# Mixer stage: the square of the state-space output behind the next chunk's decays, and GpSimd's steps in another order

## Chip, cores and metric

The program runs on one core of one Trainium2 chip. The metric is the device time of one execution in microseconds (us), the median of several runs.

## What is computed

The reference is one layer of a hybrid network over 2048 tokens of width 1024. A projection gives q, k, v, z, xbc and dt. From these a dilated attention over three patterns and a state-space mixer are formed. Their outputs go through an output projection, a convolved gated feed-forward net and a gated embedding. The change lies in the state-space mixer, which works in 16 chunks of 128 tokens, with 16 heads of width 64 in 2 groups, and a state of 128:

```python
acum = jnp.cumsum(ac, axis=2)
decay = jnp.exp(jnp.where(causal, acum[:, :, :, None] - acum[:, :, None], -jnp.inf))
cb = jnp.einsum('bclgn,bcsgn->bclsg', cc, bc)
y_diag = jnp.einsum('bclsge,bcsgep->bclgep', cb[..., None] * decay, xc)
chunk_states = jnp.einsum('bclgn,bclgep->bcgepn', bc, xc * decay_to_end[..., None])
# over the chunks: h = h * chunk_decay + chunk_state
y_off = jnp.einsum('bclgn,bcgepn->bclgep', cc, h_in) * jnp.exp(acum)[..., None]
y = y_diag + y_off + d_skip[:, None] * xs
y = y * silu(z)
return rms_norm(y, norm_g)
```

The norm at the end needs the sum of y squared over the 1024 inner channels of each token.

## The kernel before, in words

The kernel has six stages: input projection, mixers, output projection, up projection, down projection and gated embedding. `mixers` (L1502) runs two programs side by side, `Attention` (L593) and `Ssd` (L1101). Each engine has a generator of each program. A generator yields a due time ahead of each group of instructions, and `weave` (L585) issues next whatever has the smallest due time. So the order in each engine's queue is fixed at build time by a plan. A group whose due time is smaller than one already issued from the same generator follows at once. An engine executes its queue in order; a semaphore wait holds all that is behind it.

**The plan.** In `Ssd`, `at(c, x)` (L1147) is 10 + 23.5 (c + x), in microseconds of the plan, so a chunk c has 23.5. In `Attention` there are four rounds r, with a first pass (maxima of the scores, 32 each) and a second pass (exponentials and value products, 75 each), in the order of L609: first passes 0 and 1, second 0, first 2, second 1, first 3, second 2 and 3. A second pass has 40 steps; step k is due at k/43 of its 75 on TensorE and at (k + 0.6)/43 on ScalarE (L842). Real time runs slower than the plan: the 16 chunks take about 35 us each.

**One chunk c of the mixer.**

- ScalarE: sixteen decays, one per head (L1288, Relu of the row of cumulative sums minus its own), after each eight of them an exponential of the group (L1293, made of 1024 columns), due from c - 0.5 on. The copy of B in token order (L1299) out of PSUM, which waits for TensorE's transposes (`turned_b`), is due at c - 0.28. The square of y (`square`, L1310, with L1314) waits for y_out and for GpSimd's additions of the chunk before, and is due at c + 0.64. In `scalar` the square of chunk c stands ahead of the decays of chunk c + 1 (due from c + 0.5).
- TensorE: `turn` (L1442) transposes x and B and forms the products of C and B (L1454, L1461, L1463), due at c - 0.32 and c - 0.2. `outputs` (L1466) forms the part from the state (L1476) and the part inside the chunk (L1485). `states` (L1488, product L1498) forms the chunk's state out of xde and the B copy, due at c + 0.9 and c + 0.98.
- VectorE: `front` (L1364) scales x by dt (L1373), masks the C-B product (L1380) and multiplies it into the decays (L1384). `outcome` (L1387) scales and adds the two parts (L1394, L1398; the second raises y_add). `carry` (L1400, L1407) adds the chunk's state to the decayed one; it is queued behind the next chunk's `front`.
- GpSimd (`gpsimd`, L1215): xde, which is x dt times the decay to the end (L1240); D times x into y (L1248), which waits for the store of the last y, for its square (sq_s) and for x; the decay of the state (L1254); y plus the sum of the two parts (L1259); y times z (L1262, raises y_out); and `add_up` (L1224), three halving additions of the squares (L1230), which waits for the square.
- SP's queue (`sync`, L1153): the load of x of chunk c + 2, which waits for D times x (dx_s, L1189) and for TensorE; the load of the cumulative rows of chunk c + 2; y's store (L1204, after y_out); z and e_cum of later chunks. The attention's loads stand in the same queue.

**Attention on the same engines.** In a second pass each step has two or more score products on TensorE (L1044 to L1046, L1049 to L1053) into one of two PSUM banks, an exponential on ScalarE (L849) and value products (L1077 to L1097). The score of step g waits for the exponential of step g - 2, the value products for the last exponential they read. The sums of a value step are added by VectorE (L928 to L936). In a first pass VectorE takes maxima (L886, L892) and ScalarE has nothing to do.

At the end TensorE sums the squares over the channels (L1438), which waits for all 16 `add_up`, and ScalarE takes the root (L1306).

Of the kernel before, what the change touches and what calls it, by code (L numbers as in the profile page):

```python
# [5 lines left out]
ALU = mybir.AluOpType  # L6
# [6 lines left out]
P = 128  # L13
SEQ, D = 2048, 1024
KD = D // P
TT = SEQ // P
# [3 lines left out]
SH, SP_, SN, SG = 16, 64, 128, 2  # L20
# [84 lines left out]
class Norm:  # L105
# [43 lines left out]
    def scalar(self, act, w_hi, w_in_s, whi_done):  # L149
        self.high_weights(act, 0, w_hi, w_in_s, whi_done)  # L150
        act.wait_ge(self.param, 16)
        for n in range(NB):
            if n == 0:
                act.wait_ge(self.first_in, 16)
            for k in range(KD):
                if k == (KD // 2 if n == 0 else 0):
                    act.wait_ge(self.loaded[n % 2], 16 * (n // 2 + 1))
                act.activation(self.hi[:, k, n * 512:(n + 1) * 512], self.x[n % 2][:, k], ACT.Copy,
                               scale=self.g[:, k:k + 1]).then_inc(self.hi_done, 1)
            if n == 0:  # L160
                self.high_weights(act, 1, w_hi, w_in_s, whi_done)
            else:
                self.take_root(act, n - 1)
            act.activation(self.sq[:, :, :], self.x[n % 2][:, :, :], ACT.Square).then_inc(self.squared, 1)
        self.take_root(act, NB - 1)
# [935 lines left out]
class Ssd:  # L1101
# [113 lines left out]
    def gpsimd(self, pool):  # L1215
        yield self.at(0, -1.6)
        pool.memset(self.one[:, :], 1.0).then_inc(self.consts, 1)
        pool.memset(self.state[0][:, :, :], 0.0).then_inc(self.consts, 1)
        pool.memset(self.eps[:, :], EPS).then_inc(self.consts, 1)
        pool.wait_ge(self.consts, 3)  # L1220
        pool.affine_select(out=self.upper[:, :], in_=self.one[:, :], compare_op=ALU.is_ge, fill=0.0, base=0,
                           pattern=[[1, P]], channel_multiplier=-1).then_inc(self.consts, 1)

        def add_up(c):  # L1224
            pool.wait_ge(self.sq_s, c + 1)
            for n, half in enumerate((4, 2, 1)):
                if c + n > 0:
                    pool.wait_ge(self.added, 3 * c + n)
                out = self.y_sq[:, 0:half] if half > 1 else self.y_sums[:, c * P:(c + 1) * P].unsqueeze(1)
                pool.tensor_tensor(out, self.y_sq[:, 0:half], self.y_sq[:, half:2 * half], ALU.add).then_inc(self.added, 1)  # L1230

        for c in range(TT):
            b = c % 2
            yield self.at(c, 0.04)
            pool.wait_ge(self.xdt_s, 2 * c + 2)
            if c > 0:
                pool.wait_ge(self.st_mm, 2 * c)
            else:
                pool.wait_ge(self.par_s, 1)
            pool.tensor_tensor(self.xde[:, :, :], self.xdt[b][:, :, :],  # L1240
                               self.to_end[:, c].unsqueeze(2).broadcast_to([P, SH, SP_]), ALU.mult).then_inc(self.xde_s, 1)
            yield self.at(c, 0.1)
            pool.wait_ge(self.xbc_in[b], 16 * (c // 2 + 1))
            pool.wait_ge(self.param, 64)
            if c > 0:
                pool.wait_ge(self.stored, 16 * c)
                pool.wait_ge(self.sq_s, c)
            pool.tensor_tensor(self.y[:, :, :], self.xbc[b][:, 0:INNER // P],  # L1248
                               self.d_col[:, :].unsqueeze(2).broadcast_to([P, INNER // P, P]), ALU.mult).then_inc(self.dx_s, 1)
            yield self.at(c, 0.2)  # L1250
            if c > 0:
                pool.wait_ge(self.state_s, 2 * c)
                pool.wait_ge(self.off_mm, 2 * c)
            pool.tensor_tensor(self.state[1 - b][:, :, :], self.state[b][:, :, :],  # L1254
                               self.chunk_decay[:, c].unsqueeze(2).broadcast_to([P, SH, SP_]), ALU.mult).then_inc(self.decayed_s, 1)
            yield self.at(c, 0.56)
            pool.wait_ge(self.y_add, 2 * c + 2)
            pool.wait_ge(self.dx_s, c + 1)
            pool.tensor_tensor(self.y[:, :, :], self.y[:, :, :], self.e_cum[b][:, :, :], ALU.add).then_inc(self.dy_s, 1)  # L1259
            pool.wait_ge(self.z_in, 16 * c + 16)  # L1260
            pool.wait_ge(self.dy_s, c + 1)
            pool.tensor_tensor(self.y[:, :, :], self.y[:, :, :], self.z[:, :, :], ALU.mult).then_inc(self.y_out, 1)  # L1262
            yield self.at(c, 0.7)
            add_up(c)

    def scalar(self, act):
        yield self.at(0, -1.4)
        act.wait_ge(self.vec, 2)
        act.activation(self.work[1], self.work[1], ACT.Exp, scale=-1.0).then_inc(self.act_s, 1)
        act.activation(self.row[:, 1], self.row[:, 1], ACT.Exp).then_inc(self.act_s, 1)  # L1270
        yield self.at(0, -1.0)
        act.wait_ge(self.cum_s, 3)
        act.activation(self.e_t, self.ps_y[:, 0:2], ACT.Exp).then_inc(self.rows_s, 1)
        act.activation(self.cum[:, :, :], self.ps_b[:, 0:2].rearrange("p a (c h) -> p (a c) h", h=SH), ACT.Copy
                       ).then_inc(self.act_s, 1)
        act.activation(self.chunk_decay[:, :, :], self.ps_o[:, 0:2].rearrange("p a (c h) -> p (a c) h", h=SH), ACT.Exp
                       ).then_inc(self.act_s, 1)
        yield self.at(0, -0.9)
        act.wait_ge(self.vec, 21)
        act.activation(self.to_end[:, :, :], self.work[2].rearrange("p (c h) -> p c h", h=SH), ACT.Exp).then_inc(self.par_s, 1)  # L1280
        for c in range(TT):
            b = c % 2
            for h in range(SH):
                if h % 2 == 0:
                    yield self.at(c, -0.5 + 0.02 * h)
                if h == 0:
                    act.wait_ge(self.cum_in[b], 16 * (c // 2 + 1))
                last = act.activation(self.m_t[b][:, h], self.m_t[b][:, h], ACT.Relu, scale=-1.0, bias=self.cum[:, c, h:h + 1])  # L1288
                if h % self.HG == self.HG - 1:
                    g, (heads, _) = h // self.HG, self.groups(h // self.HG)  # L1290
                    last.then_inc(self.seg_s, 1)
                    act.wait_ge(self.seg_s, 2 * c + g + 1)
                    act.activation(self.m_t[b][:, heads], self.m_t[b][:, heads], ACT.Exp, scale=-1.0).then_inc(self.decay_s, 1)  # L1293
                if h == self.HG - 1:
                    yield self.at(c, -0.28)
                    act.wait_ge(self.turned_b, c + 1)
                    if c >= 2:
                        act.wait_ge(self.st_mm, 2 * c - 2)
                    act.activation(self.b_tok[b][:, :, :], self.ps_b[:, 0:SG], ACT.Copy).then_inc(self.btok_s, 1)  # L1299
            yield self.at(c, 0.64)  # L1300
            self.square(act, c)
        yield self.at(TT, 0.3)
        act.wait_ge(self.summed, 1)
        act.wait_ge(self.consts, 4)
        for n, bank in enumerate((self.ps_x, self.ps_b, self.ps_y, self.ps_o)):
            last = act.activation(self.y_sums[0:1, n * 512:(n + 1) * 512], bank[0:1, :, :].rearrange("p h t -> p (h t)"),  # L1306
                                  ACT.Sqrt, bias=self.eps[0:1, 0:1], scale=1.0 / INNER)
        last.then_inc(self.rooted, 1)
# [1242 lines left out]
```

## Time and profile before

| what | value |
|---|---|
| median of 3 runs | 3347.71 us |
| lowest and highest | 3346.45 and 3350.16 us |
| profiled execution, its own time | 3352.7 us |
| its span | 3351.0 us |
| mean granted TensorE clock | 0.968 |
| TensorE (PE) busy | 3160.5 us, 94% |
| VectorE (DVE) busy | 1630.4 us, 49% |
| ScalarE (ACT) busy | 818.2 us, 24% |
| GpSimd (POOL) busy | 227.8 us, 7% |

The profile is of one execution. Its span runs from the first to the last instruction; its own time holds a little more around it. Busy times are sums of instruction durations of an engine (PEld is TensorE's weight load). In a timeline row stand the start in us, the duration in us, the engine, the line, the operation, what it writes and reads, and the count of instructions merged; in brackets the idle time of the engine before it and what ended it. The duration of merged rows runs to the end of the last one.

### The profile page before, as it was taken

How to read it: one execution, taken by the hardware profiler on the slowest of the kernel's cores; microseconds unless marked ns; L12 is line 12 of the kernel's file. 1: busy time of each engine (PE TensorE's matmuls, PEld its weight loads, DVE VectorE, ACT ScalarE, POOL GpSimd, SP SyncE). 2: the span in 40 equal slices, each digit the busy share in tenths (PEclk: the TensorE clock that was granted, in tenths of full speed). 3: DMA queues.
4: the chain of work that ended last, by engine and by line, in shares of the span. 5: the costliest groups of instructions: out<-in, count | busy, mean ns of one | idle time of the engine just before them, and what ended most of it. 6: DMA issues, size and time to landing. Idle time of an engine off the chain costs nothing. (4 is left out here: it accounts for less than half of the span.)

```text
span 3351.0 us, 37968 instructions
## 1 busy us (share of the span) xinstructions
PE 3160.5 (94%) x15525; PEld 2477.0 (74%) x15590; DVE 1630.4 (49%) x1562; ACT 818.2 (24%) x1148; POOL 227.8 (7%) x182
## 2 busy tenths in 40 slices
PE   7899999968988888899899999999999899999899
PEld 5678888745555555678778888888888788788687
DVE  7864552145555543633464554444555532532643
ACT  5221121113343433311311111111111422321421
POOL 0000000003333332000000000000000000000000
PEclk9999999978988999999999999999999999999999
DMA  3222222247465561534311111111111624424542
GB/s 133 94 107 70 75 71 80 75 117 172 129 190 137 164 165 52 189 128 144 136 50 50 41 38 47 50 50 50 50 50 50 220 107 181 158 107 146 153 142 69
DMA packets 228401, 354.90 MB, mean 106 GB/s; under 512 B 38049, under 2 KB 123041, under 8 KB 220737
## 3 DMA queue, kind: packets, MB, share of 16 engines
q1 hardware_dynamic: 224578, 333.39, 31.8%
q0 software_dynamic: 3712, 19.96, 1.6%
q8 instruction: 78, 1.28, 0.2%
q14 instruction: 33, 0.27, 0.0%
HBM read 256.08 MB, written 96.84 MB: 105 GB/s over the span
## 5 line engine op out<-in xcount | busy, mean ns | idle before, releaser
L90 PE MATMUL up_ps<-up_h_hi,up_w_hi 128*128 128x512 f32 x1408 | 550.1, 391 | 7.3 <-DVE up_h_lo L1784 7.3
L91 PE MATMUL up_ps<-up_h_lo,up_w_hi 128*128 128x512 f32 x1408 | 548.7, 390 | 0.0
L92 PE MATMUL up_ps<-up_h_hi,up_w_lo 128*128 128x512 f32 x1408 | 548.7, 390 | 0.0
L90 PE MATMUL inp_ps<-inp_h_hi,carry_q 128*128 128x512 f32 x896 | 353.8, 395 | 12.3 <-DVE inp_h_lo L189 9.5
L91 PE MATMUL inp_ps<-inp_h_lo,carry_q 128*128 128x512 f32 x896 | 349.7, 390 | 0.0
L92 PE MATMUL inp_ps<-inp_h_hi,carry_k_two 128*128 128x512 f32 x896 | 349.6, 390 | 0.0
L90 PEld LDWEIGHTS up_ps<-up_h_hi,up_w_hi 128*128 128x128 f32 x1408 | 265.0, 188 | 64.1 <-issue 9.1
L91 PEld LDWEIGHTS up_ps<-up_h_lo,up_w_hi 128*128 128x128 f32 x1408 | 264.9, 188 | 55.8 <-issue 0.7
L92 PEld LDWEIGHTS up_ps<-up_h_hi,up_w_lo 128*128 128x128 f32 x1408 | 264.8, 188 | 55.0
L1929 DVE TENSOR_TENSOR carry_squares<-up_ps,carry_rows 128x2048 f32<-128x2048 f32 x42 | 96.2, 2292 | 420.8 <-PE up_ps L92 420.4
L90 PE MATMUL down_banks<-down_a_hi,down_w_hi 128*128 128x512 f32 x704 | 277.1, 394 | 14.7 <-DVE down_a_lo L2155 12.4
L91 PE MATMUL down_banks<-down_a_lo,down_w_hi 128*128 128x512 f32 x704 | 276.0, 392 | 0.0
L92 PE MATMUL down_banks<-down_a_hi,down_w_lo 128*128 128x512 f32 x704 | 275.7, 392 | 0.0
L90 PEld LDWEIGHTS inp_ps<-inp_h_hi,carry_q 128*128 128x128 f32 x896 | 169.0, 189 | 50.9 <-issue 11.7
L1939 DVE SCALAR_TENSOR_TENSOR carry_room<-carry_squares,up_cw,carry_room 128x2048 f32<-128x2048 f32 x84 | 197.5, 2352 | 3.0
L91 PEld LDWEIGHTS inp_ps<-inp_h_lo,carry_q 128*128 128x128 f32 x896 | 168.9, 189 | 36.9 <-issue 1.9
L92 PEld LDWEIGHTS inp_ps<-inp_h_hi,carry_k_two 128*128 128x128 f32 x896 | 168.8, 188 | 35.2
L90 PE MATMUL outp_banks<-outp_m_hi,outp_w_hi 128*128 128x512 f32 x384 | 152.6, 397 | 22.2 <-DVE outp_m_lo L1646 15.8
L90 PEld LDWEIGHTS down_banks<-down_a_hi,down_w_hi 128*128 128x128 f32 x704 | 133.4, 189 | 45.7 <-issue 18.1
L92 PEld LDWEIGHTS down_banks<-down_a_hi,down_w_lo 128*128 128x128 f32 x704 | 133.4, 190 | 28.2
L91 PEld LDWEIGHTS down_banks<-down_a_lo,down_w_hi 128*128 128x128 f32 x704 | 133.4, 190 | 27.6
L91 PE MATMUL outp_banks<-outp_m_lo,outp_w_hi 128*128 128x512 f32 x384 | 151.9, 396 | 0.0
(318 smaller groups left out, 4647.4 us busy)
## 6 DMA issues: line engine op xcount, KB each, us to landing
carry_room<-in_w_up_dram SPq DMA_DIRECT2D x42, 512.0 KB, 5.7
act<-carry_room SPq DMA_DIRECT2D x21, 1024.0 KB, 4.6
carry_room<-act SPq DMA_DIRECT2D x7, 2816.0 KB, 13.3
down_a_second<-act SPq DMA_DIRECT2D x7, 2816.0 KB, 18.4
carry_room<-cum_rows SPq DMA_DIRECT2D x16, 1024.0 KB, 6.2
carry_room<-x SPq DMA_DIRECT2D x8, 2048.0 KB, 9.3
carry_room<-in_w_in_dram SPq DMA_DIRECT2D x26, 512.0 KB, 6.0
xbc<-carry_room SPq DMA_DIRECT2D x12, 1024.0 KB, 5.7
```

Source lines behind the costliest of these rows:

```text
L90: pe.matmul(out, w_hi, x_hi, start=first, stop=False)
L91: pe.matmul(out, w_hi, x_lo, start=False, stop=False)
L92: return pe.matmul(out, w_lo, x_hi, start=False, stop=last)
L1929: dve.tensor_tensor(pre[b][:, 2:2 + SEQ], ps[b][:, :], norm.rstd[:, :], ALU.mult).then_inc(pre_s, 1)
L1939: dve.scalar_tensor_tensor(out=conv[b], in0=pre[b][:, c:c + SEQ], scalar=cw[:, b, c:c + 1], in1=conv[b], op0=ALU.mult, op1=ALU.add).then_i ...
```

## The change

In ScalarE's program the square of chunk c - 1 is issued at c - 0.2, after the decays of chunk c, and no longer at 0.64 of its own chunk ahead of them; the last square is issued at 15.8. In GpSimd's program the decay of the state comes right after xde, then `add_up` of the chunk before, then D times x; `add_up` no longer ends the chunk, and the last one is issued at 15.9. The instructions and the semaphores are the same.

```diff
@@ gpsimd
             yield self.at(c, 0.1)
+            if c > 0:
+                pool.wait_ge(self.state_s, 2 * c)
+                pool.wait_ge(self.off_mm, 2 * c)
+            pool.tensor_tensor(self.state[1 - b][:, :, :], self.state[b][:, :, :],
+                               self.chunk_decay[:, c].unsqueeze(2).broadcast_to([P, SH, SP_]), ALU.mult).then_inc(self.decayed_s, 1)
+            yield self.at(c, 0.2)
+            if c > 0:
+                add_up(c - 1)
             pool.wait_ge(self.xbc_in[b], 16 * (c // 2 + 1))
             pool.wait_ge(self.param, 64)
             if c > 0:
...
                 pool.wait_ge(self.sq_s, c)
             pool.tensor_tensor(self.y[:, :, :], self.xbc[b][:, 0:INNER // P],
                                self.d_col[:, :].unsqueeze(2).broadcast_to([P, INNER // P, P]), ALU.mult).then_inc(self.dx_s, 1)
-            yield self.at(c, 0.2)
-            if c > 0:
-                pool.wait_ge(self.state_s, 2 * c)
-                pool.wait_ge(self.off_mm, 2 * c)
-            pool.tensor_tensor(self.state[1 - b][:, :, :], self.state[b][:, :, :],
-                               self.chunk_decay[:, c].unsqueeze(2).broadcast_to([P, SH, SP_]), ALU.mult).then_inc(self.decayed_s, 1)
             yield self.at(c, 0.56)
...
             pool.tensor_tensor(self.y[:, :, :], self.y[:, :, :], self.z[:, :, :], ALU.mult).then_inc(self.y_out, 1)
-            yield self.at(c, 0.7)
-            add_up(c)
+        yield self.at(TT, -0.1)
+        add_up(TT - 1)
@@ scalar
                     act.activation(self.b_tok[b][:, :, :], self.ps_b[:, 0:SG], ACT.Copy).then_inc(self.btok_s, 1)
-            yield self.at(c, 0.64)
-            self.square(act, c)
+            if c > 0:
+                yield self.at(c, -0.2)
+                self.square(act, c - 1)
+        yield self.at(TT, -0.2)
+        self.square(act, TT - 1)
```

## Rows read from the trace of the kernel before

**Rows 1.** The page: busy time, share of the span and instructions of each engine

```profile
PE 3160.5 (94%) x15525; PEld 2477.0 (74%) x15590; DVE 1630.4 (49%) x1562; ACT 818.2 (24%) x1148; POOL 227.8 (7%) x182
```

**Rows 2.** Busy us by stretch: PE, PEld, DVE, ACT, POOL; granted clock, DMA share, GB/s

```profile
757.00:1310.00 553.00, 487.56 (x3863) 312.73 (x3922) 287.34 (x366) 204.83 (x453) 205.16 (x128) 0.91 0.56 148
```

**Rows 3.** Who waited for whom, 757 to 1310 us: total, times, longest in us

```profile
ACT mix_y_sq L1314 <- POOL mix_y L1262: 122.2, 16, 28.3
...
PE mix_a_banks L1044 <- ACT mix_probs L849: 24.8, 10, 5.5
PE mix_ps_x L1498 <- DVE mix_state L1407: 8.8, 7, 5.5
PE mix_a_banks L1095 <- ACT mix_probs L849: 8.1, 3, 3.8
PE mix_a_banks L1045 <- ACT mix_probs L849: 7.8, 3, 3.0
```

**Rows 4.** ScalarE's timeline, chunk 6 (start, us, instruction, idle before, releaser)

```profile
986.54 0.60 ACT L849 ACTIVATE mix_probs<-mix_a_banks 128x512 f32<-128x512 f32 x1 [1.77 <-PE mix_a_banks L1046]
989.11 1.06 ACT L1314 ACTIVATE mix_y_sq<-mix_y 128x1024 f32<-128x1024 f32 x1 [1.97 <-POOL mix_y L1262]
990.07 2.43 ACT L1288 ACTIVATE carry_room<-carry_room,mix_cum 128x128 f32<-128x128 f32 x8
992.53 1.06 ACT L1293 ACTIVATE carry_room<-carry_room 128x1024 f32<-128x1024 f32 x1
993.50 0.58 ACT L849 ACTIVATE mix_probs<-mix_a_banks 128x512 f32<-128x512 f32 x1
993.97 0.38 ACT L1299 ACTIVATE mix_b_tok<-mix_ps_b 128x256 f32<-128x256 f32 x1
```

**Rows 5.** TensorE's timeline, the same chunk

```profile
987.69 0.61 PE L1463 MATMUL mix_ps_b<-carry_room 128*128 128x128 f32 x4
...
990.29 0.39 PE L1046 MATMUL mix_a_banks<-mix_q_max,mix_k_one 65*128 65x512 f32 x1
...
994.13 0.28 PE L1044 MATMUL mix_a_banks<-mix_both_k,mix_ident_b 128*128 128x256 bf16 x1 [3.01 <-ACT mix_probs L849]
...
994.58 0.98 PE L1077 MATMUL mix_a_banks<-mix_probs,mix_v 128*64 128x256 f32 x4
...
998.31 0.61 PE L1044 MATMUL mix_a_banks<-mix_both_k,mix_ident_b 128*128 128x512 bf16 x1 [0.88 <-ACT mix_probs L849]
...
1003.55 0.65 PE L1077 MATMUL mix_a_banks<-mix_probs,mix_v 128*64 128x256 f32 x4
```

**Rows 6.** Busy time of TensorE in 11 stretches behind stops (PE busy, clock, DMA)

```profile
995.00:1001.50 6.50, 5.62 (x35) 0.50 0.16 31
...
sum 66.00, PE 60.84; mean PE 5.53
```

**Rows 7.** Timeline of all engines, chunk 4

```profile
922.51 1.06 ACT L1314 ACTIVATE mix_y_sq<-mix_y 128x1024 f32<-128x1024 f32 x1 [14.53 <-POOL mix_y L1262]
...
930.71 1.22 DVE L1384 TENSOR_TENSOR carry_room<-carry_room,mix_ps_b 128x1024 f32<-128x1024 f32 x1 [0.53 <-ACT carry_room L1293]
...
932.68 2.05 PE L1498 MATMUL mix_ps_x<-mix_xde,mix_b_tok 128*128 128x512 f32 x2 [5.54 <-DVE mix_state L1407]
```

**Rows 8.** GpSimd's timeline, chunk 10

```profile
1109.83 1.90 POOL L1240 TENSOR_TENSOR mix_xde<-mix_xdt,mix_to_end 128x1024 f32<-128x1024 f32 x1 [7.69 <-PE mix_ps_x L1498]
1111.69 1.90 POOL L1248 TENSOR_TENSOR mix_y<-carry_room,mix_d_col 128x1024 f32<-128x1024 f32 x1
...
1121.29 2.40 POOL L1259 TENSOR_TENSOR mix_y<-mix_y,carry_rows 128x1024 f32<-128x1024 f32 x1 [5.85 <-DVE carry_rows L1398]
```

**Rows 9.** Timeline of all engines, the end of the mixer

```profile
1306.70 2.08 POOL L1230 TENSOR_TENSOR mix_y_sq<-mix_y_sq 128x512 f32<-128x512 f32 x2 [1.17 <-ACT mix_y_sq L1314]
...
1308.85 0.46 POOL L1230 TENSOR_TENSOR mix_y_sums<-mix_y_sq 128x128 f32<-128x128 f32 x1
...
1320.81 1.02 PE L1438 MATMUL mix_ps_x<-mix_y_sums,mix_one 128*1 128x512 f32 x2
```

## Prediction

> **What bounds the kernel now.** I start with how full TensorE is. It works 94% of the span [rows 1], so only what makes TensorE stand still, or run slower, can be won. The change touches one stage alone, the mixer. From 757 to 1310 us TensorE is busy for 487.56 of 553 us there at a mean granted clock of 0.91 [rows 2]: 65 us stand idle, and part of the rest runs at the low clock. Next comes who made TensorE wait in that stretch [rows 3]. The longest sums are waits for ScalarE's exponentials of the attention scores (L849), 24.8, 8.1 and 7.8 us in 16 waits, 40.7 us together. Then come 8.8 us of waits for VectorE's state additions (L1407), 5.5 us of it at once. So the bound is TensorE, held up by ScalarE, though ScalarE works only 204.83 us of the 553: it is its order that hurts, not its load.
>
> The timeline of ScalarE shows the order [rows 4]. At 987.1 it is free, but the next instruction in its queue is the square of y (L1314), which waits for GpSimd until 989.11. Behind the square stand decays that became due meanwhile (eight L1288 in 2.43 us, L1293 1.06 us), and the exponential comes only at 993.50. TensorE shows the other side [rows 5]: its last score product ends at 990.68, some transposes follow to 991.1, and it stands still for 3.01 us, then 0.88 us more. After the stop its matmuls are slow: the four L1077 take 0.98 us where they take 0.65 us at 1003.55, and the granted clock from 995 to 1001.5 is 0.50, the 1.2 GHz level of the two [rows 6]. I find such a stop in each of the 12 chunks whose squares have exponentials behind them (chunks 1, 2, 3, 5 to 8 and 10 to 14), and after most of them a stretch at the low clock.
>
> **The change, part by part.** I worked out the order of ScalarE's queue by sorting the due times of the two programs (an exponential is due every 1.74 us of the plan, a chunk every 23.5).
>
> *The square.* Before: square, 8 decays and their exponential, one score exponential, the B copy, 8 decays and exponential. After, in chunk 6's case: 4 decays, score exponential, 4 decays and exponential, two score exponentials, B copy, 8 decays and exponential, one score exponential, square. The same instructions run, so the load stays; what goes is the wait for y_out ahead of score exponentials, and the first block of 1.06 + 2.43 + 1.06 = 4.6 us is broken up. Walk of that chunk, from [rows 4, 5]: the first four decays lie in an earlier hole, the other four and their exponential (1.2 + 1.06 us) in the 1.77 us ahead of 986.54, which they overrun by 0.5; the score exponential due at 986.54 ends near 987.65, the next near 988.25. The B copy starts as the transposes end at 988.3, and 0.38 + 2.43 + 1.06 us later, at 992.1, the next score exponential starts and ends near 992.7. TensorE needs that one for a score that comes after one short score product (0.5 us) and a group of value products (1.7 us; with one long score product of 0.9 they fill 988.3 to 990.68, less an overlap), which start at 991.1, so at 993.3. No stop is left, and y_out came at 989.1, before the square's new place at 992.7. From 991.1 TensorE then has a short score product, the values, and twice a long score product and a state pair (1.0 us in part beside the next, so 0.6; the pair takes 2.05 at the low clock, [rows 7]): 0.5 + 1.7 + 2 x (0.9 + 0.6) = 5.2 us, and is near 996.3 at the point it had at 1003.55: 7.2 us, of which 3.9 are the two stops and 3.3 the clock. That chunk is better than the mean; where the B copy and its decays meet a TensorE with less in hand I leave 0.8 us of stop in each of 12 chunks, 10 us. Term: 40.7 - 10 = 30.7 us. Bounds: 0 and 40.7.
>
> *The state additions.* In chunk 4 no exponentials are near, yet the square waits 14.53 us, the decays end at 930.69, VectorE's product with them starts at 930.71, the state addition only after it, and TensorE stands 5.54 us [rows 7]. After the change these decays stand ahead of the square and need only the transposes. I take 4 us; bounds 0 and 8.8 [rows 3], and I take less than half because VectorE's maxima of the first attention pass stand between the steps there.
>
> *The clock.* The 11 stretches behind these stops cover 66 us with TensorE busy for 60.84 us, the walked chunk's at a clock of 0.50 [rows 6] and the others within 0.05 of it. If all of that doubled its speed it would give 30 us; if the clock stayed low, 0. In the walked chunk it is half of the stretch, but strided score products hardly depend on the clock, so I take 0.3 of 66 = 20 us and leave 5 us for stops that remain: 15 us.
>
> *GpSimd.* Its order becomes xde, state decay, addition of the last chunk's squares (2.08 + 0.46 us, [rows 9]), D times x. No instruction is added; D times x ends 1.9 + 1.9 + 2.6 + 1.9 = 8.3 us after the start of xde. The cover is the wait for y's sum: in the tightest chunk xde starts at 1109.83 and y's addition at 1121.29 [rows 8], 11.5 us later, so 3.2 us are left and the cost is nothing. If that cover went, each late microsecond would go into y_out, then into the square and into SP, which holds the load of x for chunk c+2 until D times x is done, with the decays' rows, y's store, z and the attention's loads behind it in SP's queue. No DMA is moved past another. D times x also waits for the square, now after the decays: that stands ahead of TensorE's state products, after which xde starts, so it is there. The state decay comes earlier, which nobody waits for.
>
> *The tail.* The last square moves behind three more score exponentials. Its sums end at 1309.31 now, some 4 us later then, and TensorE uses them at 1320.81 [rows 9]: nothing.
>
> Sum: 30.7 + 4 + 15 = 49.7, say 50 us. The profiled execution took 3352.7 us around a span of 3351.0, that is 3302.7 after; it is 5 us above the median of the runs, 3347.7, so the median goes to 3297.7. If every bound came true it would be 40.7 + 8.8 + 30 = 79.5 us.
>
> **The rivals.** *A, the next limit takes most of it.* VectorE works 287 us in the stage and the DMA share is 0.56 on average [rows 2]; both crowd into the stretches of the first attention pass. If the low clock also stays, only the stops go, and half of them come back as waits for VectorE's maxima or late loads. 20 us are left: 3327.7. Against it: in the 12 chunks concerned the stops are put down to ScalarE alone. *B, nothing happens.* The B copy now waits for transposes, and 8 decays stand behind it: the stop moves there with the same 3.4 us (40.7 over 12), 3347.7. *C, slower.* The block in the second half, B copy, 8 decays, exponential and then the square soon after, is 0.38 + 2.43 + 1.06 + 1.06 = 4.9 us. If TensorE had nothing in hand there but one score product of 0.9 us, it would stand still for 4.9 + 0.6 - 0.9 = 4.6 us in each chunk in place of 3.4, so 12 x 1.2 = 14 us more: 3362. It decides where TensorE has less than 2.1 us of work in hand, since 4.9 + 0.6 - 2.1 is today's 3.4. Against B and C stands the walked chunk, where TensorE has 5.0 us (988.3 to 993.3), and the second block of today, which costs only 0.88 us there though TensorE came to it late.
>
> *D, GpSimd's chain gets too long.* If VectorE held up each of the four steps once, for the 1.22 us of its product [rows 7], D times x would end 4.9 us later, 1.7 us beyond the cover, and in the three tightest chunks that costs 5 us: 3302.7. Against it: the steps take 1.90 us each [rows 8] with VectorE at work beside them. The Trainium skill (SBUF — State Buffer, Who interferes with whom) has the rule for such a hold: a VectorE instruction with two SBUF inputs and a GpSimd one that reads SBUF exclude each other. The rows here show no such hold, and VectorE's product in them has one input in PSUM.
>
> **How the numbers follow.** My forecast has 0.71, D 0.05, A 0.14, B 0.04, C 0.06. A measurement of this kernel tells a change from none at about 0.2%, 7 us. Faster by more: 0.71 + 0.05 + 0.14 = 0.90; the same 0.04; slower 0.06. The range from 3274 (a gain of 74, near the bounds' sum) to 3327 (A) leaves out C, B and the extremes, some 2 in 10.
>
> **What would show it.** Right: ScalarE's wait at the square falls from 122.2 us [rows 3] to a few in the chunks with exponentials; TensorE's waits for L849 in the mixer fall from 40.7 to about 10 us; the stretches at 1.2 GHz behind them go; the mixer stage ends some 50 us earlier, and everything behind it takes the same time. Wrong: waits for L849 of the same sum but with the B copy and decays ahead of them (B, C); waits for VectorE or DMA in their place (A); GpSimd's y addition no longer waiting for VectorE's sum but starting right behind D times x (D). The clock term is wrong if the stops vanish and the clock still falls.

## The result, and the profile after

The changed kernel takes 3307.25 us (median of 4 runs, 3304.45 to 3307.49) beside 3348.37 us of the kernel before in the same session (3346.45 to 3350.16): 41.1 us less, a ratio of 0.9875 with a 95% interval of 0.9858 to 0.9892. In a second session it took 3304.42 us beside 3350.49 us, a ratio of 0.9854 (0.9828 to 0.9879). So it is faster by 1.3 to 1.5%; 3297.7 us was forecast, with a range of 3274 to 3327.

The two profiled executions are further apart than the medians: 3352.7 us before, 3307.44 us after, 45.3 us. The page of the changed kernel, busy time by engine (against [rows 1]):

```profile
PE 3149.2 (95%) x15525; PEld 2470.4 (75%) x15590; DVE 1629.0 (49%) x1562; ACT 817.6 (25%) x1148; POOL 227.6 (7%) x182
```

The instructions are the same in number; TensorE is busy for 11.3 us less, and the other engines hold their sums.

**Where the 45.3 us come from.** A tile's view gives for each line the shortest, median and longest duration in ns, and then the first and the last start in us. Two lines frame the mixer on TensorE: the first transposes of x, and the last value products of the attention. Before:

```profile
L1454 PE MATMUL mix_ps_x<-mix_ident,carry_room x128: 270/272/476, 750.3 to 1277.6; 128*128 128x128 f32 x128
...
L1095 PE MATMUL mix_a_banks<-mix_probs,mix_v x256: 272/273/476, 887.6 to 1335.8; 128*64 128x128 f32 x128
```

After:

```profile
L1459 PE MATMUL mix_ps_x<-mix_ident,carry_room x128: 270/272/475, 753.1 to 1231.8; 128*128 128x128 f32 x128
...
L1095 PE MATMUL mix_a_banks<-mix_probs,mix_v x256: 272/273/476, 879.1 to 1289.9; 128*64 128x128 f32 x128
```

From 750.3 to 1335.8 it is 585.5 us, from 753.1 to 1289.9 it is 536.8: 48.7 us are won in the mixer. It starts 2.8 us later in this execution; 2.4 us of that is there when the input projection, which the change doesn't touch, starts its last products (695.7 us against 693.3); and what lies behind the mixer takes 2017.5 us against 2016.9. 48.7 - 2.8 - 0.6 = 45.3. This **mixer stretch** (first start of the x transposes to last start of L1095) is the measure of all the experiments below; in two executions of the changed kernel it is 536.8 and 537.4 us, while the input projection alone ends anywhere from 690.9 to 695.9 us.

The busy time by stretch, from the first value product to the last (PE, PEld, DVE, ACT, POOL; granted clock, DMA share, GB/s). First before, then after:

```profile
807.40:1337.00 529.60, 470.87 (x3798) 300.65 (x3854) 261.33 (x344) 204.55 (x444) 186.76 (x117) 0.93 0.51 139
```

```profile
810.00:1291.00 481.00, 457.12 (x3798) 293.01 (x3854) 259.56 (x343) 203.99 (x444) 186.46 (x117) 0.96 0.56 153
```

The reader is to see two gains in these: TensorE's idle time falls from 58.7 to 23.9 us (34.8 us), and the same matmuls take 13.75 us less, while the mean granted clock goes from 0.93 to 0.96. Who made TensorE wait in that stretch, before:

```profile
PE mix_a_banks L1044 <- ACT mix_probs L849: 24.8, 10, 5.5
PE mix_a_banks L1095 <- ACT mix_probs L849: 9.8, 4, 3.8
PE mix_a_banks L1045 <- ACT mix_probs L849: 7.8, 3, 3.0
PE mix_ps_x L1498 <- DVE mix_state L1407: 7.5, 6, 5.5
...
PE mix_a_banks L989 <- DVE mix_maxima L886: 1.7, 3, 1.1
...
PE mix_ps_x L1498 <- DVE mix_xdt L1373: 0.2, 1, 0.2
```

and after:

```profile
PE mix_ps_x L1503 <- DVE mix_state L1412: 6.6, 7, 3.1
PE mix_ps_x L1503 <- DVE mix_xdt L1378: 3.8, 2, 3.7
PE mix_a_banks L989 <- DVE mix_maxima L886: 3.7, 4, 2.2
PE mix_a_banks L1044 <- ACT mix_probs L849: 2.4, 4, 1.5
...
PE mix_a_banks L1095 <- ACT mix_probs L849: 1.6, 1, 1.6
```

The waits for exponentials fall from 42.4 to 4.0 us. (The 1.6 us is the attention's last step, behind the state-space work; it was there before too, and [rows 3] end ahead of it, which is why they give 40.7 and not 42.4.) The state additions give 0.9 us, and a wait for x times dt of 3.7 us is new.

**The walked chunk.** ScalarE's timeline of chunk 6, against [rows 4]:

```profile
967.40 1.27 ACT L1290 ACTIVATE carry_room<-carry_room,mix_cum 128x128 f32<-128x128 f32 x4
968.71 1.06 ACT L1295 ACTIVATE carry_room<-carry_room 128x1024 f32<-128x1024 f32 x1
969.67 1.06 ACT L849 ACTIVATE mix_probs<-mix_a_banks 128x512 f32<-128x512 f32 x2
971.08 0.38 ACT L1301 ACTIVATE mix_b_tok<-mix_ps_b 128x256 f32<-128x256 f32 x1 [0.35 <-PE mix_ps_b L1468]
971.36 2.44 ACT L1290 ACTIVATE carry_room<-carry_room,mix_cum 128x128 f32<-128x128 f32 x8
973.83 1.06 ACT L1295 ACTIVATE carry_room<-carry_room 128x1024 f32<-128x1024 f32 x1
974.80 0.58 ACT L849 ACTIVATE mix_probs<-mix_a_banks 128x512 f32<-128x512 f32 x1
975.27 1.05 ACT L1319 ACTIVATE mix_y_sq<-mix_y 128x1024 f32<-128x1024 f32 x1
```

The square (now L1319) waits for nothing, here and in the 15 other chunks. The B copy waits 0.35 us for the transposes. From 964 to 978 us TensorE is busy for all of the 14 us, at a granted clock of 1.00, the 2.4 GHz level.

**The new stop.** The longest stop of TensorE in the mixer after the change has no counterpart before. The timeline of all engines of the changed kernel, chunk 14 (weight loads left out):

```profile
1188.13 0.59 SPq L759 DMA_DIRECT2D mix_t<-mix_o_den  x1
...
1199.24 0.69 DVE L928 COPY mix_o_den<-mix_a_banks 128x512 f32<-128x512 f32 x1 [8.15 <-DMA mix_t<-mix_o_den]
...
1199.85 0.68 DVE L1378 TENSOR_TENSOR mix_xdt<-mix_ps_x,mix_dt 128x512 f32<-128x512 f32 x1
...
1200.68 2.05 PE L1503 MATMUL mix_ps_x<-mix_xde,mix_b_tok 128*128 128x512 f32 x2 [3.66 <-DVE mix_xdt L1378]
...
1204.67 2.05 PE L1503 MATMUL mix_ps_x<-mix_xde,mix_b_tok 128*128 128x512 f32 x2 [0.67 <-DVE mix_state L1412]
```

VectorE's first value copy of the attention's last round (L928) writes the buffer whose store SP issued at 1188.13, so it waits 8.15 us for that store; x times dt, mask, products and state addition are queued behind it, and TensorE stands 3.66 and 0.67 us. From 1198.8 to 1209 the granted clock is 0.51. The same wait was there before, hidden (VectorE's and TensorE's timelines of the kernel before):

```profile
1240.13 0.69 DVE L928 COPY mix_o_den<-mix_a_banks 128x512 f32<-128x512 f32 x1 [6.26 <-DMA mix_t<-mix_o_den]
```

```profile
1241.05 0.61 PE L1044 MATMUL mix_a_banks<-mix_both_k,mix_ident_b 128*128 128x512 bf16 x1 [4.64 <-ACT mix_probs L849]
```

It ended at 1240.1, inside a stop of TensorE that ScalarE made.

### The profile page after: what moved, and what is told of

It reads as the page before. It is cut to its first block and busy times, and to the rows that moved or that the text cites. A ratio compares the mean times of both kernels' runs of the same rounds, so it can differ in the third digit from the quotient of the medians.

```text
span 3305.7 us, 37968 instructions
## 1 busy us (share of the span) xinstructions
PE 3149.2 (95%) x15525; PEld 2470.4 (75%) x15590; DVE 1629.0 (49%) x1562; ACT 817.6 (25%) x1148; POOL 227.6 (7%) x182
```

## The experiments

My theory: the whole gain is ScalarE's, and most of it is the wait for the mixer's output ahead of the exponentials, not the length of what ScalarE does there; GpSimd's order is worth nothing; what is missing in the mixer is the stop behind the store. Ten runs tell this apart, one of them the changed kernel again. All medians of one session share the runs of the kernel before named with them. "Waits" are TensorE's waits for L849 in the mixer.

| kernel | median us | ratio to before, 95% | mixer stretch | waits |
|---|---|---|---|---|
| before | 3348.37 | | 585.5 | 42.4 |
| changed | 3307.25 | 0.9875 (0.9858 to 0.9892) | 536.8 | 4.0 |
| act_only | 3301.32 | 0.9844 (0.9828 to 0.9861) | 538.8 | 3.9 |
| pool_only | 3352.11 | 0.9996 (0.9986 to 1.0007) | 587.1 | 42.9 |
| no_wait | 3312.31 | 0.9885 (0.9869 to 0.9902) | 542.4 | 14.8 |
| burst | 3307.07 | 0.9867 (0.9851 to 0.9884) | 536.3 | 10.9 |
| after_again | 3304.42 | 0.9854 (0.9828 to 0.9879) | 537.4 | 4.1 |
| late_copy | 3298.39 | 0.9846 (0.9829 to 0.9863) | 530.1 | 4.1 |
| cover_1 | 3305.53 | 0.9868 (0.9850 to 0.9886) | 538.7 | 3.9 |
| cover_3 | 3304.39 | 0.9867 (0.9851 to 0.9883) | 536.9 | 4.0 |
| late_two | 3294.11 | 0.9829 (0.9815 to 0.9842) | 524.1 | 4.0 |
| late_act | 3295.51 | 0.9829 (0.9814 to 0.9844) | 531.3 | 4.0 |

The kernel before took 3352.35 us beside the first four experiments, 3350.49 beside the next four and 3352.88 beside the last two.

### act_only and pool_only: each half alone

act_only is the kernel before with the change in `scalar` only; pool_only the changed kernel with this taken back:

```diff
-            if c > 0:
-                yield self.at(c, -0.2)
-                self.square(act, c - 1)
-        yield self.at(TT, -0.2)
-        self.square(act, TT - 1)
+            yield self.at(c, 0.64)
+            self.square(act, c)
```

> The kernel before with ScalarE's part of the change alone: the squares of a chunk stand behind the next chunk's decays, GpSimd keeps its old order. If ScalarE's order is all of the gain (my theory), the time is that of the changed kernel within its scatter, 3307 us give or take 5, and TensorE waits on the score exponentials for under 10 us in all in the mixer. If GpSimd's earlier decay of the state brings a part (the rival), the time lies clearly above, 3320 us or more, with longer waits for state additions.

> The changed kernel with ScalarE's squares back at their old place, so that GpSimd's part alone is left. My theory: the time of before, 3348 us give or take 5, with TensorE waiting some 40 us on the score exponentials again. The rival, that GpSimd's order brings a part of its own, gives under 3335 us.

ScalarE's half alone gives 3301.32 us and a mixer stretch of 538.8 us, GpSimd's alone 3352.11 us and 587.1. Beside 3352.35 of the kernel before the second is nothing, to 0.1% either way. TensorE's longest waits in pool_only, from 757 to 1310 us as in [rows 3], are the old ones (with the attention's last step, behind 1310 us, the second sum of L849 is 9.8 us):

```profile
PE mix_a_banks L1044 <- ACT mix_probs L849: 33.1, 14, 5.5
PE mix_ps_x L1500 <- DVE mix_state L1409: 8.8, 7, 5.5
PE mix_a_banks L1095 <- ACT mix_probs L849: 8.2, 3, 3.8
```

The reader is to see the 5.5 us state addition too: GpSimd's order leaves it as it was. In act_only it is 3.1 us, so what goes of it goes with the decays that no longer stand behind the waiting square. The median of act_only is lower than that of the changed kernel, but their intervals meet at 0.986, and the mixer stretch is not shorter; so this says no more than that GpSimd's half is worth nothing.

### no_wait and burst: the wait, or the run of decays

In the old order a score exponential stood behind a wait and behind a block of 4.6 us. no_wait takes the wait from the kernel before and leaves the block; it leaves out the squares of y (it squares ones in their place):

```diff
-        act.wait_ge(self.y_out, c + 1)
...
-        act.activation(self.y_sq[:, :, :], self.y[:, :, :], ACT.Square).then_inc(self.sq_s, 1)
+        act.activation(self.y_sq[:, :, :], self.one[:, :].unsqueeze(1).broadcast_to([P, INNER // P, P]), ACT.Square).then_inc(self.sq_s, 1)
```

burst is the changed kernel with a chunk's first eight decays due together:

```diff
-                    yield self.at(c, -0.5 + 0.02 * h)
+                    yield self.at(c, max(-0.36, -0.5 + 0.02 * h))
```

> The kernel before with the squares at their old place, but reading a constant tile in place of the mixer's output: ScalarE waits for nothing there, and as many instructions are issued as before. It leaves out the squares of y, so the norm's sums are not those of the reference. What is left of the old order is the run of decays ahead of the score exponentials. Old waits on exponentials: 40.7 us. If the wait for the outputs is all of the loss, the time is 3307 us; if the run of decays without exponentials between them is all of it, 3345 us. I expect mostly the wait: 5 to 15 us of waits on exponentials are left, and 3310 to 3330 us.

> The changed kernel with the decays of a chunk all due at once, so that the run of eight decays and their exponential stands in one piece on ScalarE, with the squares still behind them. The wait for the outputs is gone and the run of decays is there. If a run of some 3 us ahead of a score exponential is enough to stop TensorE, 3320 us or more, with waits on exponentials of 15 us or more; if the wait for the outputs was what mattered, 3307 to 3315 us. I expect the second.

no_wait wins 43.1 of the 48.7 us in the mixer, burst all of them. ScalarE's timeline of no_wait in chunk 6 shows the block without a wait:

```profile
969.78 0.60 ACT L849 ACTIVATE mix_probs<-mix_a_banks 128x512 f32<-128x512 f32 x1 [1.77 <-PE mix_a_banks L1046]
970.27 1.05 ACT L1315 ACTIVATE mix_y_sq<-mix_one 128x1024 f32<-128x1024 f32 x1
971.22 2.44 ACT L1288 ACTIVATE carry_room<-carry_room,mix_cum 128x128 f32<-128x128 f32 x8
973.69 1.06 ACT L1293 ACTIVATE carry_room<-carry_room 128x1024 f32<-128x1024 f32 x1
974.65 0.58 ACT L849 ACTIVATE mix_probs<-mix_a_banks 128x512 f32<-128x512 f32 x1
```

and TensorE's stops there, the only ones of 0.3 us or more from 960 to 985:

```profile
975.29 0.28 PE L1044 MATMUL mix_a_banks<-mix_both_k,mix_ident_b 128*128 128x256 bf16 x1 [0.93 <-ACT mix_probs L849]
...
979.46 0.39 PE L1044 MATMUL mix_a_banks<-mix_both_k,mix_ident_b 128*128 128x512 bf16 x1 [2.06 <-ACT mix_probs L849]
```

The old block of 4.6 us costs 0.93 us where with the wait in front it cost 3.01 [rows 5]. Most of the block alone lies beside TensorE's own work; at this first stop the wait in front of it, 1.97 us in that chunk [rows 4], goes to TensorE in full: 3.01 - 0.93 = 2.08 us. The second stop grows meanwhile from 0.88 to 2.06 us, so both together fall by 0.90 us only. What is gained besides is the clock: 1.00 from 979.5 to 986.5 us, where it was 0.50 from 995 to 1001.5 us of the kernel before [rows 6].

So the block is not free. Over the mixer no_wait has 10.8 us more of waits for exponentials than the changed kernel, and 32.4 us of idle TensorE in place of 23.9 (58.7 before). That its stretch is only 5.6 us longer is because its matmuls take 5.0 us less (452.1 against 457.1 us). Nor has it the changed kernel's stops of 3.66 and 0.67 us in chunk 14; there it has 0.83, 1.72 and 2.21 us.

Without the square in front (burst) the first stop is gone and the 2.06 us one stays; its stretch is no longer than the changed kernel's all the same. One difference is at chunk 14, where burst's TensorE stands 1.72, 1.69 and 0.72 us and not 3.66 and 0.67.

### late_copy: the stop behind the store

VectorE's first value copy of the attention's last round is due 2.6 steps of the attention later, which puts it behind the chunk's x times dt, mask and products in VectorE's queue. All else is the changed kernel:

```diff
-                yield self.in_step(r, self.last_step(h + 1) + 1.3)
+                yield self.in_step(r, self.last_step(h + 1) + (3.9 if (r, h) == (KVH - 1, 0) else 1.3))
```

> The changed kernel unaltered, once more, as the yardstick of this batch: 3307 us give or take 5 as in its first runs. In the trace a stop of TensorE of some 4 us near 1200 us, behind a VectorE copy that waits for the store of the attention's denominators.

> The changed kernel with VectorE's first value copy of the last attention round due 2.6 steps later, so that it stands behind the chunk's x times dt, mask, products and first state addition in VectorE's queue, and not ahead of them. My theory: the stop near 1200 us (3.7 and 0.7 us idle, then 10 us at the lower clock) comes from that copy, which waits 8 us for a store. Then the stop goes, and the kernel is 5 to 9 us faster than the changed kernel beside it: about 3299 us. The rival: the copy is needed just as early, TensorE waits for the values in its place, and the time stays at 3307 us or rises.

The stretch falls by 7.3 us against after_again, the median by 6.0. The same place in the timeline of all engines:

```profile
1196.82 1.02 PE L1503 MATMUL mix_ps_x<-mix_xde,mix_b_tok 128*128 128x512 f32 x2
...
1199.49 1.29 DVE L928 COPY mix_o_den<-mix_a_banks 128x512 f32<-128x512 f32 x2 [0.92 <-DMA mix_t<-mix_o_den]
...
1200.32 0.65 PE L1077 MATMUL mix_a_banks<-mix_probs,mix_v 128*64 128x256 f32 x4 [0.51 <-DVE mix_o_den L928]
```

The store lands no sooner. The copy still starts at 1199.5, but x times dt and the products are done by then, the state products run at 1196.82 and not at 1200.68, and the value products wait 0.51 us. The granted clock from 1196 to 1206 is 1.00 where it was 0.51. 4.3 us of stop cost 7.3 us of time.

### cover_1 and cover_3: how much cover GpSimd has

The prediction gave GpSimd 3.2 us of cover. These kernels issue D times x once or three times more in every chunk (1.9 or 5.7 us):

```diff
+            for k in range(3):
+                pool.tensor_tensor(self.y[:, :, :], self.xbc[b][:, 0:INNER // P],
+                                   self.d_col[:, :].unsqueeze(2).broadcast_to([P, INNER // P, P]), ALU.mult).then_inc(self.cover, 1)
+                pool.wait_ge(self.cover, 3 * c + k + 1)
```

> The changed kernel with one more D times x (1.9 us) on GpSimd ahead of the counted one in every chunk. The prediction gave GpSimd 3.2 us of cover in its tightest chunk, so it should cost nothing: 3307 us give or take 5. If GpSimd's chain is at its limit (the rival), TensorE or the store of y is held in most of 16 chunks, 3320 us or more. The extra instructions also take SBUF time beside VectorE: if GpSimd held VectorE back, VectorE's own instructions would be longer by their share.

> The changed kernel with three more D times x (5.7 us) on GpSimd in every chunk, more than the 3.2 us of cover of the tightest chunk. By the prediction the final products of the tightest chunks come 2.5 us later, and with them the squares, which now stand behind the next decays and can bear some of it: 3307 to 3315 us. If the cover is what the prediction's rows show and its loss lands on TensorE at full price, some 2.5 us in up to 6 chunks, 3315 to 3325 us. If GpSimd has no part in the bound at all, 3307 us.

Neither costs anything: stretches of 538.7 and 536.9 us. That 5.7 us is more than the cover shows in GpSimd's timeline of cover_3, chunk 10:

```profile
1082.07 5.85 POOL L1257 TENSOR_TENSOR mix_y<-carry_room,mix_d_col 128x1024 f32<-128x1024 f32 x3
1088.00 1.90 POOL L1260 TENSOR_TENSOR mix_y<-carry_room,mix_d_col 128x1024 f32<-128x1024 f32 x1
1090.04 2.38 POOL L1265 TENSOR_TENSOR mix_y<-mix_y,carry_rows 128x1024 f32<-128x1024 f32 x1
1092.57 2.38 POOL L1268 TENSOR_TENSOR mix_y<-mix_y,carry_room 128x1024 f32<-128x1024 f32 x1
```

The addition to y follows D times x with no wait (in [rows 8] it waited 5.85 us), so the chain is now the bound of y_out in that chunk. It still delays nobody: y is complete at 1094.95, and the square, at its new place, starts only at 1097.27.

### late_two and late_act: more of the same, and the best version

In late_copy the longest stop that is left behind a DMA is at 1072.22, for the maxima. In VectorE's timeline an addition of the denominators stands in front, which waits for their transfer (VectorE's row first, TensorE's second):

```profile
1070.51 0.19 DVE L942 TENSOR_TENSOR mix_den_fold<-mix_den_fold 128x32 f32<-128x32 f32 x1 [3.19 <-DMA mix_den_fold<-mix_o_den]
```

```profile
1072.22 1.03 PE L989 MATMUL mix_a_banks<-mix_low_q,mix_ident_b 128*128 128x512 bf16 x2 [2.74 <-DVE mix_maxima L886]
```

late_two puts it later as well, and with it the store on SP's queue that waits for it:

```diff
-            yield self.at(2, r, 1.0) + self.OUT
+            yield self.at(2, r, 1.0) + self.OUT + (5.0 if r == 1 else 0.0)
...
-            yield self.at(2, r, 1.0) + self.OUT + 1.0
+            yield self.at(2, r, 1.0) + self.OUT + (6.0 if r == 1 else 1.0)
```

> late_copy with, besides, VectorE's inverses of the second attention round (and the store of them on SP) due 5 planned us later. In the trace of late_copy VectorE waits 3.2 us at 1070.5 for the fold of the denominators, and TensorE then stops 2.7 us for maxima behind it and goes on at the lower clock. If a stop costs itself and a stretch at half clock whatever makes it, as the one near 1200 us did (4.3 us of stop, 7.3 us of time), this one is worth 4 to 7 us more: about 3293 us. The rival: the transfer of the fold is late on its own account, or VectorE is so full there that TensorE waits for maxima all the same: the time of late_copy, 3298 us.

> late_copy with GpSimd in its old order, so that of the change ScalarE's part alone is left. If GpSimd's part is worth nothing (as ScalarE's part alone and GpSimd's part alone showed), the time of late_copy, 3298 us give or take 5. The rival, that GpSimd's new order does harm (ScalarE's part alone measured 3301 us and the whole change 3304 to 3307 us), gives 3293 us or less.

late_two takes 3294.11 us, and its stretch is 6.0 us shorter than that of late_copy. From 1068 to 1083 us the granted clock rises from 0.66 (late_copy, first row) to 0.89 (late_two, second):

```profile
1068.00:1083.00 15.00, 12.04 (x48) 5.96 (x48) 10.39 (x13) 1.64 (x2) 2.61 (x2) 0.66 1.05 322
```

```profile
1068.00:1083.00 15.00, 14.15 (x85) 9.52 (x85) 12.80 (x17) 0.93 (x1) 8.07 (x6) 0.89 1.02 297
```

It has the lowest median of all versions, and its stretch is the shortest; it is the change and two of VectorE's due times, with the store that goes with one. But the medians alone do not show that the second due time is worth something: late_copy's interval (0.9829 to 0.9863) overlaps that of late_two (0.9815 to 0.9842), and late_act, without that due time, has the same ratio, 0.9829. What shows it is the profile, one of each kernel: the stop is gone and the stretch is 6.0 us shorter, where two profiles of one kernel differed by 0.6. late_act, with GpSimd in its old order, has late_copy's stretch (531.3 against 530.1 us): once more GpSimd's order is worth nothing, and does no harm either.

## Why the prediction was right, and where it was off

The direction was right, and the path too: the gain is in the mixer, in TensorE's waits for exponentials and in the clock behind them. In the mixer 49.7 us were forecast and 48.7 measured. That the two are so near is in part luck: the terms err in both directions, by up to 7.6 us each, and cancel:

- **The exponentials:** 30.7 us forecast, 38.3 measured (40.7 to 2.4, without the last step). The 0.8 us of stop left in each of 12 chunks was too careful: the B copy and its decays find TensorE with enough in hand in all of them. Within a second pass the B copy waits at most 1.93 us; where one begins, in chunk 5, it waits 8.89 us for the transposes, and TensorE stops 1.49 us behind it, the longest that is left. The walk of chunk 6 was right step by step.
- **The state additions:** 4 us forecast, 0.9 measured. In chunk 4 the stop falls from 5.54 [rows 7] to 3.09 us, as foreseen for its cause: there VectorE is busy almost without a break from 905 to 920 with maxima, mask and products, and the addition comes last. The prediction named those maxima as its reason to take less than half, and still took too much. Elsewhere these waits grew from 2.0 to 3.5 us, 0.67 of it behind the store.
- **The clock:** 15 us forecast, 13.75 measured. Luck here too: 5 of an estimate of 20 us were kept back for stops that would remain, and hardly any did; in their place came the new stop, which cost 3.0 us of clock (7.3 - 4.3).
- **New waits:** none in the sum, about 4 us measured (x times dt 3.6 and L886 2.0 more, L892 1.6 less). This is the step that failed. The prediction asked who is late next for ScalarE alone, by giving each chunk a remainder. At the stop at 1241.05 VectorE stood too, behind a store, to 1240.1. That row was in the trace of before, as were its queue and its 6.26 us. late_copy priced it: 7.3 us with the clock. The 2.0 us more behind L886 are of the same kind: in the changed kernel VectorE stands 2.64 us at 1070.39 for the transfer of the denominators, ahead of TensorE's stop of 2.19 us at 1072.11. In the kernel before this addition came at 1100.24 and did not wait at all, so the gain itself made this wait.
- **GpSimd and the tail:** nothing forecast, nothing measured. The real cover is larger than 3.2 us, since past it comes the square's own slack. The last sums are there at 1264.9 and are used at 1273.7.

The median came out 9.6 us above the forecast though the mixer was right within 1 us, and the rest lies outside of the change. The prediction took the profiled execution to be 5 us above the median and moved the forecast down by it. In three later sessions the kernel before had medians of 3350.5 to 3352.9 us, so it was the median of the first three runs that was low. The input projection takes 681.5 to 686.4 us from one profile to another, in kernels that do not differ there; between the two profiles compared here it is 2.3 us more for the changed kernel.

**The rivals.** B and C fall with ScalarE's timeline: the decays behind the B copy stop TensorE nowhere for more than 1.5 us. D falls with cover_3: even 5.7 us more on GpSimd are free. A came true in part: another engine's wait took over at one place, with 7.3 us and not 30. It was a store's wait, and not the load of VectorE.

**What stays open.** Why burst, with 7 us more of waits for exponentials than the changed kernel, is not slower: its matmuls take 3.8 us less (453.3 against 457.1 us), and at chunk 14 its stop is split in three, with a clock of 0.83 from 1200 to 1210 us against 0.56. What sets the clock there was not tried, nor in no_wait, whose matmuls take 5.0 us less. So what the block of decays costs by itself is not settled: 10.8 us of waits in no_wait, and some of it comes back in the clock. Not tried either are the stop of 3.09 us in chunk 4 and the 13.4 us at the start of the output projection, where TensorE waits for VectorE in both kernels.

## What to carry to other kernels

In an in-order queue a wait brings its own length and, in one block behind it, all the work that came due meanwhile (in chunk 6 a wait of 1.97 us and a block of 4.6 us stopped TensorE for 3.01 us, the block alone for 0.93), so put a step that waits for another engine's late result behind the work that others wait for; the square lost nothing by coming a chunk later. Before such a stop is counted as won, look at what every other engine waits for inside of it, DMA waits above all: of the two that mattered here one was hidden in such a stop and the other came only because the work behind came earlier, and with two groups of VectorE's put later the mixer stretch was 13 us shorter. And in a kernel whose untouched stages move by 5 us from run to run, compare the touched stretch from landmark to landmark.

## What the runs showed of the hardware

Stops of like length were followed by different clocks. Behind the stop of 2.06 us in no_wait (979.46) the clock from 979.5 to 986.5 is 1.00, and behind the same one in burst it is 1.00 as well; behind the changed kernel's stop of 2.19 us (1072.11) it is 0.50 from 1074 to 1082. TensorE had other work ahead of them, score and value products in the one case and first-pass scores, which wait for maxima again and again, in the other. So the prediction's share per stretch came near in the sum (13.75 against 15 us) and would not have for a single stop.

GpSimd beside VectorE: with 48 more instructions of D times x, VectorE's means stay where they were, by line in the mixer of cover_3 (48 more) and, behind it, of the changed kernel:

```profile
L1393 DVE TENSOR_TENSOR carry_room<-carry_room,mix_ps_b 128x1024 f32<-128x1024 f32 x32 | 38.5, 1216 | 1.7
```

```profile
L1389 DVE TENSOR_TENSOR carry_room<-carry_room,mix_ps_b 128x1024 f32<-128x1024 f32 x32 | 38.5, 1216 | 1.7
```

The addition of L931 has 1126 ns against 1125. Both have one input in PSUM. An instruction of VectorE with both inputs in SBUF fares otherwise. One such in the mixer is the short addition of the denominators (L942). GpSimd's and VectorE's rows in burst, and then VectorE's in late_two, where GpSimd stands still:

```profile
1214.02 1.90 POOL L1256 TENSOR_TENSOR mix_y<-carry_room,mix_d_col 128x1024 f32<-128x1024 f32 x1
```

```profile
1214.59 1.37 DVE L942 TENSOR_TENSOR mix_den_fold<-mix_den_fold 128x32 f32<-128x32 f32 x1
```

```profile
1202.76 0.18 DVE L942 TENSOR_TENSOR mix_den_fold<-mix_den_fold 128x32 f32<-128x32 f32 x1
```

Alone it takes 0.18 or 0.19 us. In burst GpSimd had begun a product before it, and the addition ends at 1215.96, 0.04 us after the end of that product at 1215.92: it was held for 1.2 us. The twelve profiles have 48 of these additions. 16 of them take 0.24 to 1.37 us, and each of those began while an instruction of GpSimd ran and ends 0.04 or 0.05 us after that one. There are only four in a kernel, so it costs little here. The Trainium skill (SBUF — State Buffer, Who interferes with whom) keeps the exclusive hold for VectorE instructions with both inputs in SBUF beside a GpSimd instruction that reads SBUF, and for VectorE's two-port modes; the rows agree on the first, the 1.37 us above against 0.18, and on instructions with one input in PSUM, which are not held (1216 ns in both kernels). No run here tried the two-port modes.
